# Product 0 of each phase's first pair made in fp32, and another order for the first norms

## The reference

```python
x += W_o( g_a * P_a(attention(n)) + g_b * P_b(RG-LRU(n)) )      # n = RMSNorm(x)
x += (silu(gate) * up) @ w_down                                 # gate, up = RMSNorm(x) @ w_gate_up
```

## Time and profile before

| | |
|---|---|
| median of 3 runs | 1644.11 us (1642.67 to 1645.88) |
| the profiled execution's own time | 1644.76 us |
| its span, first to last instruction | 1643.0 us |
| mean granted TensorE clock | 0.993 of full speed |
| TensorE matmul busy | 1607.5 us, 98% |
| VectorE busy | 1027.6 us, 63% |
| GpSimd busy | 997.6 us, 61% |
| ACT busy | 644.0 us, 39% |

### The profile page before, as it was taken

The page is one execution under the profiler, slowest core; times in us unless marked ns, Lnnn a source line. Parts: engine busy times, 40 slices in busy tenths (PEclk is TensorE's granted clock), DMA queues, the critical chain, the costliest instruction groups (busy, mean ns, idle before and its releaser), DMA issues. The chain is left out here.

```text
span 1643.0 us, 28698 instructions
## 1 busy us (share of the span) xinstructions
PE 1607.5 (98%) x11338; PEld 1540.7 (94%) x11338; DVE 1027.6 (63%) x1717; ACT 644.0 (39%) x1322; POOL 997.6 (61%) x714
## 2 busy tenths in 40 slices
PE   7999999999999999999999999999999999999998
PEld 4999999989999898899899989999999999998998
DVE  7677556865646556768798895333333335868695
ACT  5535552354444535424334443333333334333231
POOL 4645543434425251497868529777777778786876
PEclk9999999999999999999999999999999999999999
DMA  5111123213122131373443312222242222373634
GB/s 193 39 52 65 64 72 99 80 66 114 66 97 66 53 114 49 130 291 123 165 149 132 131 39 103 80 78 79 79 184 79 79 79 79 139 271 130 233 142 152
DMA packets 73033, 182.10 MB, mean 111 GB/s; under 512 B 15092, under 2 KB 26676, under 8 KB 72260
## 3 DMA queue, kind: packets, MB, share of 16 engines
q1 hardware_dynamic: 52228, 160.35, 27.7%
q10 hardware_dynamic: 20672, 19.93, 3.8%
HBM read 131.23 MB, written 49.28 MB: 110 GB/s over the span
## 5 line engine op out<-in xcount | busy, mean ns | idle before, releaser
L642 PE MATMUL bank<-xh,wsh 128*128 128x264 f32 x2170 | 620.1, 286 | 8.4 <-DVE spare L1862 3.8
L642 PE MATMUL bank<-xh,wsl 128*128 128x264 f32 x2170 | 616.8, 284 | 0.0
L642 PE MATMUL bank<-xl,wsh 128*128 128x264 f32 x2170 | 616.0, 284 | 0.0
L642 PEld LDWEIGHTS bank<-xh,wsh 128*128 128x128 f32 x2170 | 408.3, 188 | 11.3 <-issue 8.0
L642 PEld LDWEIGHTS bank<-xl,wsh 128*128 128x128 f32 x2170 | 408.4, 188 | 0.2
L642 PEld LDWEIGHTS bank<-xh,wsl 128*128 128x128 f32 x2170 | 408.4, 188 | 0.0
L642 PE MATMUL bank<-acth,wh 128*128 128x352 f32 x960 | 319.3, 333 | 5.6 <-POOL wl L546 4.1
L642 PE MATMUL bank<-acth,wl 128*128 128x352 f32 x960 | 314.7, 328 | 0.0
L642 PE MATMUL bank<-actl,wh 128*128 128x352 f32 x960 | 314.3, 327 | 0.0
L618 POOL TENSOR_TENSOR wsl<-praw,wsh 128x512 fp32r<-128x512 f32 (+1 forms) x157 | 247.6, 1577 | 70.6 <-ACT wsh L1284 70.4
L544 POOL TENSOR_SCALAR wh<-wraw 128x512 fp32r<-128x512 f32 (+1 forms) x100 | 70.9, 709 | 311.9 <-PE bank L642 292.9
(11 more groups left out here) (187 smaller groups left out, 2428.1 us busy)
## 6 DMA issues: line engine op xcount, KB each, us to landing
praw<-in_weights SPq DMA_DIRECT2D x34, 1024.0 KB, 5.0
wraw<-in_weights SPq DMA_DIRECT2D x52, 512.0 KB, 3.3
h_scratch<-ev SPq DMA_DIRECT2D x44, 264.0 KB, 2.1
acc<-h_scratch SPq DMA_DIRECT2D x4, 2112.0 KB, 12.6
ev<-x_scratch SPq DMA_DIRECT2D x6, 1056.0 KB, 5.0
spare<-x_scratch SPq DMA_DIRECT2D x6, 1056.0 KB, 4.9
praw<-in_weights SPq DMA_DIRECT2D x8, 768.0 KB, 5.3
ta_scratch<-tg ACTq DMA_DIRECT2D x24, 176.0 KB, 1.9
```

The source lines that it names most:

```text
L642: return nc.tensor.matmul(*args, **kw)
```

## The change

In the FP32 table phases 1, 2, 4, 5 and 6 get product 0 too, so that of their first pair only product 1 is split. `copy_back` comes at product 1 of the second pair, not at product 0. In the first norms, TensorE's sum of squares for group 1 comes after one more raw block; ACT takes a root of eight ones per row, into a buffer that isn't read, before the squares of group 1, and the roundings of group 0 are divided by the root of group 1; VectorE makes the sums of group 1 in another grouping, with the reciprocal of group 0 among them, and those of group 2 in the midst of the norms of group 0.

```diff
@@ -149,7 +149,7 @@
 PLAIN = PHASE_FIRST[GATE_UP]
 PLAIN_ORDER = ((0, 0, 0), (0, 0, 1), (0, 1, 1), (0, 1, 0), (1, 0, 1), (1, 1, 1), (1, 0, 0), (1, 1, 0))
 PLAIN_BANKS = {(0, 0): 2, (1, 1): 0, (0, 1): 4, (1, 0): 6}
-FP32 = ((0, 1, 2, 3, 4, 5, 6), (2, 3, 4, 5, 6), (2, 3, 4, 5, 6), (0, 2, 3, 4, 5, 6)) + ((2, 3, 4, 5, 6),) * 3
+FP32 = ((0, 1, 2, 3, 4, 5, 6),) + ((0, 2, 3, 4, 5, 6),) * 6
 X_FIRST = tuple(f + (f == PLAIN) for f in PHASE_FIRST[:PHASES])
 BANKS = ((0, 1), (4, 5), (2, 3), (6, 7), (0, 1), (4, 5), (6, 7))
 LOWS = ((0, 1, 2, 3, 4, 5, 6),) * 3 + ((1, 0, 2, 3, 4, 5, 6),) + ((0, 1, 2, 3, 4, 5, 6),) * 3
@@ -700,8 +700,8 @@
                     raw_block(0, 0)
                     sumsq(0)
                     raw_block(0, 1)
+                    raw_block(0, 2)
                     sumsq(1)
-                    raw_block(0, 2)
                     raw_block(1, 0)
                     sumsq(2)
                     raw_block(1, 1)
@@ -1007,12 +1007,14 @@
                 f(wg[:, 0, c * P:(c + 1) * P], wraw[:, 0, c * P:(c + 1) * P], ACT.Identity, scale=vt[:, c, V_G1:V_G1 + 1])\
                     .then_inc(wg01_done[0], 1)
             squares(0)
+            f(qstd[:, 0, 0:KC], ones[:, 0:KC], ACT.Sqrt)
             squares(1)
             root(0)
             squares(2)
             rstd_row(0)
+            high(0, range(0, 4))
             root(1)
-            high(0, range(KC))
+            high(0, range(4, KC))
             rstd_row(1)
             high(1, range(0, 4))
             root(2)
@@ -1399,7 +1401,7 @@
                             w_high(*made)
                     for made in x_after.get((p, r), ()):
                         x_high(*made)
-                    if r == 0 and p - 1 in (X_FIRST[ATTN_OUT], X_FIRST[OUT]):
+                    if r == 1 and p - 1 in (X_FIRST[ATTN_OUT], X_FIRST[OUT]):
                         copy_back(p - 1)
                     if p == PLAIN - 1 and r == 3:
                         scale_weights()
@@ -1483,12 +1485,18 @@
             for c in range(KC):
                 V.tensor_scalar(wg[:, 1, c * P:(c + 1) * P], wraw[:, 1, c * P:(c + 1) * P], vt[:, c, V_G1:V_G1 + 1], None, ALU.mult)\
                     .then_inc(wg01_done[1], 1)
-            chunk_sum(1, 0, KC, 2)
+            q = xsq[:, 1, :, :]
+            dve.wait_ge(xsq_done, 3)
+            vec(V.tensor_tensor(q[:, 0:2, :], q[:, 0:2, :], q[:, 2:4, :], ALU.add))
             rstd(0)
+            dve.wait_ge(xsq_done, 4)
+            vec(V.tensor_tensor(q[:, 4:6, :], q[:, 4:6, :], q[:, 6:8, :], ALU.add))
+            vec(V.tensor_tensor(q[:, 0:2, :], q[:, 0:2, :], q[:, 4:6, :], ALU.add))
+            V.tensor_tensor(xsum[:, 2, :], q[:, 0, :], q[:, 1, :], ALU.add).then_inc(xchunk_done, 1)
             norm(0, range(0, 4))
+            chunk_sum(2, 0, KC, 3)
+            norm(0, range(4, KC))
             rstd(1)
-            norm(0, range(4, KC))
-            chunk_sum(2, 0, KC, 3)
             norm(1, range(0, 4))
             rstd(2)
             norm(1, range(4, KC))
```

## The result

The changed kernel takes 1649.03 us (median of 9 runs, 1647.49 to 1651.39), the kernel before 1644.11 beside it: a ratio of 1.0032, 95% interval 1.0024 to 1.0041. It is slower by 0.32% by this ratio, and by 4.9 us between the two medians. The forecast was 1646.8 and its range, 1642.5 to 1650.0, holds the result; but the outcome that I had called likeliest, the same within 0.2%, is not what came.

What follows compares the result with a forecast made beforehand. TensorE, busy 1607.5 of 1643.0 us, was taken as the bound, with VectorE and a DMA the path in ATTN_OUT. Terms +0.5 + 0.2 + 0.64 + 0.48 + 0.9 = +2.7 us over the 1644.11 median: 1646.8, range 1642.5 to 1650.0.

Steps and rivals of the forecast that it cites:

- 0.5 for ATTN_OUT and OUT together: Where ATTN_OUT and OUT begin: 1.3 us later in the first less 0.8 gained in the second, +0.5.
- 1.3 for DOWN: The three DOWN phases: +0.2 in DOWN 1, +0.64 and +0.48 in DOWN 2 and 3.
- 0.9 for the start: First 55 us: VectorE's moved sums meet GpSimd's weight splits, low parts end at 53.7 instead of 52.80, +0.9.
- I take 1.3 later: ATTN_OUT: the VectorE and GpSimd chain behind the held-back x_sum 2 comes 1.3 us later, arriving at OUT.
- the change doesn't touch: Lower-clock stretches, 1.2 of 2.4 GHz, four of 3.4 or 6.8 us: claimed unaffected; 3.4 us more or less is about 1.4.
- the 2.14: TensorE's wait for GpSimd at 798.70 in pair 5, 2.14 us: claimed to go but buy nothing.
- my bound of 2.3: Upper bound on ATTN_OUT's delay, 2.3 us (760.35 less 758.06); the lower was 0.
- rival (b): The waits come back: 2.1 stays won in ATTN_OUT and the start gains; -3.4, 1640.7, faster; chance 0.1.
- -0.8: OUT: one VectorE delay of 0.96 us goes with GpSimd's subtraction, taken as 0.8 gained; bounds 0 and 1.9.
- 0.64 and 0.48: DOWN 2 and 3: unsplit product 0's full price on TensorE, nothing won and nothing waiting, +0.64 and +0.48.
- Rival (a): DOWN 1's residual load makes combine 3 of pair 34 late, about 1423.6: sum +5.4, 1649.5, slower; chance 0.25.
- The rule of the Trainium skill: Start: a two-SBUF-input VectorE instruction and a GpSimd one reading SBUF don't share; the later blocks, making the reorder a loss.

Runs made afterwards that it cites:

- `copy_at_0`: Changed kernel with ACT's copy at product 0 of the second pair, as before; 1647.91 us beside 1644.35, ratio 1.0024.
- `fetch_away`: Changed kernel with 65 short matmuls added in the first dense blocks, moving TensorE's instruction packets earlier; 1652.72 us against 1642.87, ratio 1.0062.
- `sum_last`: Changed kernel with x_sum 2 of ATTN_OUT behind combine 6 of pair 3 in VectorE's list; 1647.19 us against 1644.69, ratio 1.0013.
- `start_sums`: Kernel before with the first norms' new order, but VectorE's group 1 sums kept ahead of group 0's reciprocal; 1645.16 us against 1644.69, ratio 1.0002.
- `copy_only`: Kernel before with only ACT's copies moved to product 1; 1645.19 us beside 1644.44, ratio 1.0007.
- `out_only`: Kernel before with product 0 unsplit in OUT alone; 1642.39 us beside 1644.44, ratio 0.9995.
- `start_only`: Kernel before with only the changed order of the first norms; 1646.16 us against 1644.35, ratio 1.0009.
- `attn_split`: Changed kernel with product 0 of ATTN_OUT split as before, its copy still at product 1; 1647.40 us beside 1644.44, ratio 1.0023.

## Why the prediction was right or wrong

**The total.** The sum of +2.7 was met by the one profile, and was 2.2 short of the medians: the profile before stood 0.65 above its median, the one after 1.5 below. That the sum met the profile is luck. It had 0.5 for ATTN_OUT and OUT together, 1.3 for DOWN and 0.9 for the start; that profile has 2.0, 1.4 and -0.6.

**ATTN_OUT is the step that failed.** "I take 1.3 later" was right about x_sum 2 (1.26), and 1.3 is also what arrives where nothing else happens (1.24 in `copy_at_0` against kernels with the same clock, 1.23 in `fetch_away`). In the changed kernel the late row load lands under an instruction packet and misses a gap of GpSimd's, another 1.2 us that the prediction had no term for; and "the change doesn't touch" the stretches of low clock was false. The wait that replaced the 2.14 is 3.9 us long, and in all six profiles that have it the clock fell behind it, for 3.41 us in three and for 6.83 in three, where pair 6 takes 1.0 and 2.0 to 2.1 us longer than before. The term is 2.45 + 1.0 or 2.0 instead of 1.3, outside my bound of 2.3. That the GpSimd wait would go and buy nothing was right, and so was naming VectorE behind the load as what is late next: rival (b) did not occur.

**OUT** was mis-sized the other way: -1.45 from pair 7 to 9 (-0.90 with the copy at product 0) instead of -0.8. I had said that TensorE would still wait before product 2 of OUT; it does not.

**DOWN.** Product 0's price was right for DOWN 2 and 3: +0.65 and +0.47 where 0.64 and 0.48 stood. In DOWN 1 the forecast took 0.44 us off it for the wait at 1403.71. But the idle time in brackets was not all that this wait cost: products 0 and 1 of pair 34 took 6.57 us with it, and two such products took 5.85 without one. So 0.72 went for 0.64, and pair 34 takes 24.10 instead of 24.18. Rival (a) did not happen. VectorE and the residual load there, in the timeline of after, answer to the earlier trace rows:

```profile
1416.71 1.95 DVE L1858 TENSOR_TENSOR ev<-ev 128x528 f32<-128x528 f32 x3 [3.20 <-DMA ev<-x_scratch]
1418.57 2.35 DVE L1730 TENSOR_TENSOR acc<-acc 128x2112 f32<-128x2112 f32 x1
1420.84 0.76 DVE L1870 SCALAR_TENSOR_TENSOR ev<-bank,ev 128x264 f32<-128x264 f32 x2
```

```profile
1411.83 0.37 SPq L2060 DMA_DIRECT2D ev<-x_scratch  x1
```

All of this came as forecast. The residual load was issued 10.33 us after pair 34's start (1401.50 here, 1400.18 before), and the forecast of 1410.5 had it at 10.3. The three additions took 1.95 instead of 4.26, x_sum 3 took 2.35, and the first half of combine 3 was done at 1421.3, about one us ahead of product 6 (1422.23), where the forecast had 0.6. What I missed is a pair further on: product 6 of pair 35 waits longer for VectorE, before and after:

```profile
1442.79 0.36 PE L642 MATMUL bank<-xh,wsh 128*128 128x264 f32 x1 [0.58 <-DVE spare L1862]
```

```profile
1444.60 0.36 PE L642 MATMUL bank<-xh,wsh 128*128 128x264 f32 x1 [1.16 <-DVE spare L1870]
```

Pair 35 takes 22.00 us instead of 21.43. So DOWN 1 costs +0.48, not +0.2.

**The start.** +0.9 was forecast for every execution; it is 0 in most and 2.8 to 3.0 where the clock rises late, with 1.4 once; the mean over seven profiles is 1.0, read at 60 us. There the average held, the shape did not. The rule of the Trainium skill that I set against the reorder ("SBUF — State Buffer", section "Who interferes with whom") is borne out in the late case, with sums of 1.75, 1.18 and 1.47 us beside GpSimd's splits. The sums of 0.96, 1.84 and 0.81 us in after show that one such collision was there anyway.

**Adding up for a typical execution:** ATTN_OUT 3.5 to 4.5, OUT -1.45, DOWN 1.4 to 1.7, the start 1.0 on average: 4.4 to 5.8, against 4.9 measured. This is a sum of terms from profiles, not a measurement of its own.

Product 0 unsplit in OUT alone was the best kernel run (1642.39), 0.05% under the kernel before, which its interval doesn't tell from nothing. Its 0.9 us is read from the product spans. `sum_last`'s order with `start_sums`' start, and OUT's later copy without ATTN_OUT's, were not tried together. So whether a part of this change is worth keeping stays open.

## What to carry to other kernels

Taking away one wait in a chain that another engine drives makes a longer wait of the ones behind it: 2.14 and 0.34 us became 2.72 in `copy_only`. A longer wait can cost clock besides: here it fell behind each of six waits of 3.9 us, and behind three of five of 2.1. An operation moved ahead of its neighbour on a queue takes over the timing noise of whatever it now waits for: ask what the old order was standing behind. Where a load's landing releases VectorE among GpSimd's operations, cost it in steps of one such operation, not by the microsecond. And before a difference between two stretches is put down to an edit, look whether the granted clock was the same in both: in `copy_at_0` it made up 1.0 of 2.26 us.

## What the runs showed of the hardware that was not expected

- A packet of 16384 bytes of the queue named instruction takes 0.97 us. Where it began 3.6 to 3.8 us behind the issue of a 1056 KB load, the load landed after 6.1 to 6.4 us; where it began 4.3 to 4.5 us behind, or 5.4 us ahead, after 4.9 to 5.1.
- After a 2.1 to 2.7 us wait of TensorE the clock fell in some executions and not in others of the same code (behind 2.1 us in `out_only`, `start_sums` and `copy_at_0`, not in before and `start_only`; behind 2.7 in `attn_split` and `fetch_away`, not in `copy_only`); after 3.9 us it fell each time.
- Most of the scatter of the kernel before goes with its clock: of 35 runs beside one batch, nine with a mean granted clock of 0.992 took 1645.7 us on average, fifteen at 0.993 1644.6, six at 0.995 1640.9 and two at 0.997 1638.1. Not all of it: two at 0.991 took 1643.6, and one at 0.994 took 1641.0.
